# Block 2's mixing products as three fp32r products of split weights and inputs

## The reference, cut to what matters

```python
h = modulate(rmsnorm_2(x, norm1_g[l]), sh1, sc1)
a, naq, nak, nav, gq, gk, gv, gates = split_in(h @ w_in[l])
br_a = conv_branch(a, ...)                 # glu, 31-tap depthwise conv, layer norm, silu, @ w_conv_out
br_b = na_latent(naq, nak, nav, ...) @ w_na_out[l]      # windowed attention, 8 heads
br_c = gqa_latent(q, k, gv, ...) @ w_gqa_out[l]         # grouped attention, 8 heads
x = x + g1 * merge(br_a, br_b, br_c, gates, w_out[l])   # sum of sigmoid(gate) * branch, @ w_out
x = x + g2 * swiglu(modulate(rmsnorm_2(x, norm2_g[l]), sh2, sc2), w_ffn_in[l], w_ffn_out[l])
```

## Time and profile before

| | us |
|---|---|
| runs (3) | median 3305.6, 3302.19 to 3306.99 |
| the profiled execution | 3307.56 |
| its span, first to last instruction | 3305.8 |
| mean granted TensorE clock | 0.962 |

### The profile page before, as it was taken

How to read it: one execution, slowest core, us unless ns; L and a number is a source line. 1 busy time by engine, 2 the same in 40 slices (tenths; PEclk the granted TensorE clock), 3 DMA queues, 4 the chain that set the end, 5 groups by cost and what they waited for, 6 DMA issues and landing times.

```text
span 3305.8 us, 36114 instructions
## 1 busy us (share of the span) xinstructions
PE 3086.5 (93%) x15078; PEld 2396.2 (72%) x15078; DVE 1602.2 (48%) x2403; ACT 1034.4 (31%) x1473; POOL 360.8 (11%) x331
## 2 busy tenths in 40 slices
PE   6999888999999988999799899999999989899998
PEld 5888667888888766788565355545888867767787
DVE  6832223585863132387354244314757626253474
ACT  4422113344431211354200234312434420253342
POOL 2300010131310000032000230010000000230000
PEclk9999889999999888999899999999999999999999
DMA  6545553455554555356222120113554533322453
GB/s 197 185 148 156 191 166 128 141 187 181 180 191 121 177 167 165 102 179 203 77 90 77 55 71 28 51 51 102 183 186 158 184 106 115 107 71 89 140 179 103
DMA packets 433640, 444.98 MB, mean 135 GB/s; under 512 B 13487, under 2 KB 425256, under 8 KB 433478
## 3 DMA queue, kind: packets, MB, share of 16 engines
q1 hardware_dynamic: 427936, 434.86, 41.1%
q0 software_dynamic: 2400, 5.40, 0.7%
q10 hardware_dynamic: 3142, 2.41, 0.2%
HBM read 441.46 MB, written 1.17 MB: 134 GB/s over the span
## 4 chain that ended last, share of the span: by engine, by line
PE 83%; issue 7%; DVE 5%; ACT 4%; POOL 1%; ACTq 0%; DMA 0%; POOLq 0%; DVEq 0%
PE bank L1325 26%; PE bank L1374 20%; PE bank L1326 13%; PE bank L1384 11%; PE bank L1317 3%; PE bank L1468 1%; PE bank L1669 1%; PE bank L1475 1%; PE bank L1679 1%; PE bank L1545 1%; PE bank L1407 1%; DVE lower L1792 1%; PE bank L1305 1%; PE bank L1534 1%; POOL R L867 1%
## 5 line engine op out<-in xcount | busy, mean ns | idle before, releaser
L1325 PE MATMUL bank<-h_pair,upper 128*128 128x512 f32 x2464 | 876.8, 401 | 37.0 <-DVE h_pair L1823 18.7
L1792 DVE TENSOR_TENSOR lower<-ring,upper 128x2048 fp32r<-128x2048 f32 (+1 forms) x238 | 570.8, 2401 | 290.2 <-ACT upper L922 290.2
L1326 PE MATMUL bank<-h_pair,lower 128*128 128x256 f32 x2464 | 693.5, 281 | 0.0
L1374 PE MATMUL bank<-hT,ring 128*128 128x256 f32 (+1 forms) x2176 | 614.6, 441 | 12.4 <-DVE hT L1782 11.4
L922 ACT ACTIVATE upper<-ring 128x2048 fp32r<-128x2048 f32 (+1 forms) x238 | 441.7, 1863 | 502.8 <-PE bank L1326 502.8
L1325 PEld LDWEIGHTS bank<-h_pair,upper 128*128 128x128 f32 x2464 | 467.5, 190 | 152.6 <-issue 34.1
L1374 PEld LDWEIGHTS bank<-hT,ring 128*128 128x128 f32 x2176 | 413.8, 192 | 207.8 <-issue 151.4
L1326 PEld LDWEIGHTS bank<-h_pair,lower 128*128 128x128 f32 x2464 | 469.9, 191 | 0.2
L1325 PE MATMUL bank<-hid_pair,upper 128*128 128x512 f32 x1232 | 432.1, 396 | 0.0
L1384 PE MATMUL bank<-ring,hT 128*128 128x256 f32 (+2 forms) x1600 | 369.0, 395 | 30.2 <-ACT Q L994 19.7
L1384 PEld LDWEIGHTS bank<-ring,hT 128*128 128x128 f32 x1600 | 314.6, 205 | 80.4 <-issue 35.7
(11 more groups left out here) (256 smaller groups left out, 2722.8 us busy)
## 6 DMA issues: line engine op xcount, KB each, us to landing
ring<-in_w_ffn_in SPq DMA_DIRECT2D x154, 1024.0 KB, 5.1
ring<-in_w_ffn_out SPq DMA_DIRECT2D x56, 1024.0 KB, 5.2
ring<-in_w_in SPq DMA_DIRECT2D x50, 1024.0 KB, 5.3
ring<-in_w_mix_in SPq DMA_DIRECT2D x48, 1024.0 KB, 5.4
ring<-in_w_mod SPq DMA_DIRECT2D x48, 1024.0 KB, 5.4
ring<-in_w_ffn_out SPq DMA_DIRECT2D x28, 768.0 KB, 4.5
ring<-in_w_mix_out SPq DMA_DIRECT2D x16, 1024.0 KB, 5.3
ring<-in_w_out SPq DMA_DIRECT2D x8, 1024.0 KB, 5.3
```

Of the source, the lines that this page charges most:

```text
L1325: pe.matmul(bank[:, 0:2 * T], up[:, cols], x_pair.rearrange("p e t -> p (e t)"), start=first, stop=False)
L1326: return pe.matmul(bank[:, 0:T], low[:, cols], x_pair[:, 0, :], start=False, stop=last)
L1374: mm = pe.matmul(bank[b][:, 0:nT], w[:, c:c + 128], rhs(k), start=k == 0, stop=k == n_k - 1)
L1792: dve.tensor_tensor(f.lower(p)[:, 0:n], slot[:, 0:n], f.upper(p)[:, 0:n].bitcast(F32), ALU.subtract)\
```

## The change

Every product of block 2's mixing with a weight (projections, gates, branches, `w_out`) becomes three fp32r products: upper weight x upper input, upper x lower, lower x upper. Norm sums, scores, PV and the turnings stay as they are.

- **Weights.** The 35 mixing pieces of a layer use raw slots 0 to 2 (piece n in slot n % 3); slots 3 to 5 hold the upper parts of the same three. Piece n is loaded when piece n-3 has been used. ScalarE rounds a piece into its upper slot (`split2_up`), then the lower part is left in the raw slot by VectorE, or, for pieces 7 to 16, by GpSimd (`split2_low`, `LOW_ON_POOL`). On ScalarE and VectorE the split of piece n+3 stands behind their work on the item that piece n fills (`piece_done`); the first three are split before the norm's root.
- **Inputs.** The normed input h is scaled (VectorE), shifted and rounded (ScalarE) and its lower part left by VectorE, chunk by chunk; item 0 takes the chunks in order, for both banks. The convolution branch's silu is computed twice, rounded and whole, and subtracted. Attention's results are evicted rounded by ScalarE (`o_up_ready`), and VectorE subtracts them from the PSUM bank (`out_low`, for unit i-4 after the mask of unit i), which now gives `o_ready`. `y2` is rounded by ScalarE and subtracted by VectorE, chunk by chunk, before `w_out`.
- **Loads.** SyncE's order is now one list, `PIECES`, for the whole kernel; outside the mixing the slots go round six as before. The third probability buffer moves from `sq` to `caus`.

The core of the diff:

```diff
+MIX2_SLOTS = 3
+MIX2_PIECES = sum(n for _, n in PROJ2) + 6 * len(BRANCH2) + 4
+LOW_ON_POOL = range(7, 17)
...
+        for n, (name, i, end) in enumerate(pieces):
+            if n >= MIX2_PIECES:
+                add(name, i, layer, end, len(out) % NW)
+                continue
+            add(name, i, layer, end, n % MIX2_SLOTS)
+            up = MIX2_SLOTS + n % MIX2_SLOTS
+            out[-1].n, out[-1].up, out[-1].up_before = mixed, n % MIX2_SLOTS, held.get(up)
+            held[up] = end
+            mixed += 1
...
+            for piece in PIECES:
+                src, k, cols = source(piece.name, piece.i, piece.layer)
+                if piece.before is not None:
+                    ended(sp, piece.before)
+                sp.dma_start(slots[piece.slot][:, 0:k * cols].rearrange("p (k n) -> p k n", k=k), src)\
+                  .then_inc(landed[piece.slot], 16)
...
+        def low2_of(pos):
+
+            n = PIECES[pos].n
+            on_pool = n % MIX2_PIECES in LOW_ON_POOL
+            count = sum((m % MIX2_PIECES in LOW_ON_POOL) == on_pool for m in range(n + 1))
+            return (low2_on_pool if on_pool else low2_on_dve), count
+
+        def split2_low(eng, pos):
+
+            piece = PIECES[pos]
+            eng.wait_ge(up2_ready, piece.n + 1)
+            eng.tensor_tensor(lowers[piece.slot], slots[piece.slot], uppers2[piece.up].bitcast(F32), ALU.subtract)\
+               .then_inc(low2_of(pos)[0], 1)
...
+                for n in LOW_ON_POOL:
+                    split2_low(pool, pos + n)
...
+            def split2_up(pos):
+
+                piece = PIECES[pos]
+                has_landed(act, pos)
+                if piece.up_before is not None:
+                    ended(act, piece.up_before)
+                act.activation(uppers2[piece.up], slots[piece.slot], ACT.Copy).then_inc(up2_ready, 1)
...
-            def glu_gates(item, nT, n_items):
+            def glu_gates(item, nT, n_items, pos):
 
                 for n in range(n_items):
                     it = item + n
                     filled(act, it)
                     act.activation(glu[it % 2][:, 0:nT], pair[it % 2][0][:, 0:nT], ACT.Sigmoid)\
                        .then_inc(glu_ready, 1)
+                    if n % 2:
+                        split2_up(pos + n - 1 + MIX2_SLOTS)
+                        split2_up(pos + n + MIX2_SLOTS)
...
+                def piece_done(n, pos=pos):
+
+                    if n + MIX2_SLOTS < MIX2_PIECES:
+                        split2_up(pos + n + MIX2_SLOTS)
...
+                    piece_done(13 + 6 * b + i)
...
-                    act.activation(cout[:, c, 0:nT], cout[:, c, 0:nT], ACT.Silu,
-                                   bias=pcol("conv_ln_b_2", KC2 * layer + c),
-                                   scale=pcol("conv_ln_g_2", KC2 * layer + c)).then_inc(ln_ready, 1)
+                    for dst in (cout_up, cout):
+                        ins = act.activation(dst[:, c, 0:nT], cout[:, c, 0:nT], ACT.Silu,
+                                             bias=pcol("conv_ln_b_2", KC2 * layer + c),
+                                             scale=pcol("conv_ln_g_2", KC2 * layer + c))
+                    ins.then_inc(ln_ready, 1)
+                piece_done(17)
+                piece_done(18)
...
-                        dst = naoT if kind.startswith("na") else goT
+                        dst = nao_up if kind.startswith("na") else go_up
                         r = slice(HD * (h % 2), HD * (h % 2) + HD)
                         q0, n = (T, T) if kind.endswith("c") else (P * qt, P)
-                        out_unit((unit), i - 3, dst[r, h // 2, q0:q0 + n], r, n)
+                        out_unit((unit), i - 3, dst[r, h // 2, q0:q0 + n], r, n, o_up_ready)
                     done = woven_before(layer, i, "gate")
                     if done:
                         sigmoid_gates(*done)
+                    done = woven_before(layer, i, "branch")
+                    if done and done[1] % 2:
+                        piece_done(17 + 6 * done[0] + done[1] // 2)
                 unit += len(units)
+                piece_done(29)
+                piece_done(30)
+                for m in range(KD):
+                    act.wait_ge(y2_ready, 16 * layer + 8 + m + 1)
+                    act.activation(y2_up[:, m, 0:nT], y2[:, m, 0:nT], ACT.Copy).then_inc(y2_up_ready, 1)
+                piece_done(31)
...
+            def products3(out, w, w_cols, x, first, last):
+
+                (up, low), (x_up, x_low) = w, x
+                for n, (w_, x_) in enumerate(((up, x_up), (up, x_low), (low, x_up))):
+                    mm = pe.matmul(out, w_[:, w_cols], x_, start=first and n == 0, stop=last and n == 2)
+                return mm
...
+            def glu_pieces(item, pos, nh, n_pairs, h_before):
+
+                for n in range(n_pairs):
+                    w = [split2(pos + 2 * n), split2(pos + 2 * n + 1)]
                     for j in range(2):
-                        bank = start_item(it + j)
-                        for e in range(2):
-                            for k in range(KD):
-                                mm = pe.matmul(bank[e][:, 0:nh * T], w[e][:, k * PC + 128 * j:k * PC + 128 * (j + 1)],
-                                               hT[:, 0:nh, k, :], start=k == 0, stop=k == KD - 1)
+                        bank = start_item(item + 2 * n + j)
+                        first = n == 0 and j == 0
+                        order = [(e, k) for k in range(KD) for e in range(2)] if first else \
+                                [(e, k) for e in range(2) for k in range(KD)]
+                        for e, k in order:
+                            if first and e == 0:
+                                pe.wait_ge(h_ready, h_before + k + 1)
+                            c = k * PC + 128 * j
+                            mm = products3(bank[e][:, 0:nh * T], w[e], slice(c, c + 128), h2(nh)(k), k == 0,
+                                           k == KD - 1)
...
+                def h2_low_part(c):
+
+                    dve.wait_ge(h2_up_ready, layer * KD + c + 1)
+                    for hf in range(2):
+                        ins = dve.scalar_tensor_tensor(out=h2_low(c, hf, 1).rearrange("p a t -> p (a t)"),
+                                                       in0=h2_whole[hf][:, c, :], scalar=mod[:, layer, c, hf:hf + 1],
+                                                       in1=h2_up[:, hf, c, :].bitcast(F32), op0=ALU.add,
+                                                       op1=ALU.subtract)
+                    ins.then_inc(h_ready, 1)
+
+                for c in range(KD):
+                    for hf in range(2):
+                        ins = dve.scalar_tensor_tensor(out=h2_whole[hf][:, c, :], in0=xT[:, hf, c, :],
+                                                       scalar=mod[:, layer, 8 + c, hf:hf + 1],
+                                                       in1=root[:, hf * T:(hf + 1) * T], op0=ALU.mult, op1=ALU.mult)
+                    ins.then_inc(h_scaled, 1)
+                    if c:
+                        h2_low_part(c - 1)
+                h2_low_part(KD - 1)
...
+                def out_low(j, unit=unit, units=units):
+
+                    kind, h, qt = units[j]
+                    up, low = (nao_up, nao_low) if kind.startswith("na") else (go_up, go_low)
+                    r = slice(HD * (h % 2), HD * (h % 2) + HD)
+                    q0, n = (T, T) if kind.endswith("c") else (P * qt, P)
+                    dve.wait_ge(o_up_ready, unit - UNITS1 + j + 1)
+                    dve.tensor_tensor(low[r, h // 2, q0:q0 + n], M[3][r, 0:n], up[r, h // 2, q0:q0 + n].bitcast(F32),
+                                      ALU.subtract).then_inc(o_ready, 1)
+
+                for i in range(len(units) + 4):
                     if i < len(units):
                         na = units[i][0] == "na"
                         mask_unit((unit), i, units[i][0], chain, bias_n if na else None)
                         bias_n += na
-                    if i >= 1:
+                    if i >= 4:
+                        out_low(i - 4)
+                    if 1 <= i < len(units) + 1:
                         scale_unit((unit), i - 1, units[i - 1][0], chain)
+                    done = woven_before(layer, i, "gate")
+                    if done:
+                        piece_done(13 + 6 * done[0] + done[1])
                     done = woven_before(layer, i, "branch")
                     if done:
                         gated_branch(*done)
+                        if done[1] % 2:
+                            piece_done(17 + 6 * done[0] + done[1] // 2)
...
+                for m in range(KD):
+                    dve.wait_ge(y2_up_ready, KD * layer + m + 1)
+                    dve.tensor_tensor(y2_low[:, m, 0:nT], y2[:, m, 0:nT], y2_up[:, m, 0:nT].bitcast(F32),
+                                      ALU.subtract).then_inc(y2_split, 1)
+                for n in range(4):
```

(3 more changed lines are left out.)

302 lines of the change are left out of this document (168 added, 134 removed).

## The result

| | before | after |
|---|---|---|
| median of 4 runs, us | 3303.89 (3298.53 to 3306.99) | 3460.16 (3459.18 to 3464.08) |
| ratio, 95% interval | | 1.0477 [1.0459, 1.0495] |
| the profiled execution, us | 3307.56 | 3460.09 |
| its span, us | 3305.8 | 3458.3 |
| mean granted TensorE clock | 0.962 | 0.908 |

The account below looks back on a forecast made before the run. TensorE, busy 93% of the span, was taken as the limit. Stage terms of +34 us in layer 0 and +75 in layer 1 made +109 on 3307.6, so 3417, or 3415 as a median; range 3335 to 3460.

Parts of the forecast that it names:

- the twelve terms: Six stages of each layer's mixing, glu to output: +34 us in layer 0, +75 in layer 1.
- the price of the products: Mixing's weight products on TensorE: 0.23 us per 512-column fp32r product, 0.12 per 256-column one, 139 us off TensorE.
- the bounds of 0.215 and of 0.19 a weight load: Product price limits: 0.215 adds 23 us of gain; 0.19 takes 155 us away (rival at 3520, chance 0.05).
- the lock between GpSimd and VectorE: Beside the convolution, GpSimd's subtractions cost VectorE 4.3 us a piece, 43 us for ten.
- T + 142 and T + 111: Convolution's end in layers 0 and 1, counted from item 3's end T; stage changes of -9 and 0 us.
- the rival of 3495: GpSimd gets no turn during the convolution, so pieces from 7 on come after it: +51 and +29 us, chance 0.07.
- `out_low` behind the mask behind the subtraction: Attention, when a gate piece ends: PV waits for VectorE's `out_low`, 14.4 against 9.7 on the step's clock, 4.7 us lost.
- The rival in which `out_low` is in time: Attention: `o_ready` comes before TensorE finishes its step's work; 121 us less than forecast, 3294, chance 0.08.
- the slow-clock term: Attention: one 3.3 us stretch at half clock after each stall, 1.7 us lost, +14 us a layer.
- its 4.15: Attention steps with nothing woven in: score, mask, `out_low`, PV in line take 4.15 us instead of 3.04.
- the range's upper end: Whole kernel: the stated range, 3335 to 3460, ended at 3460 and left 0.20 out.
- the forecast's own band: Whole kernel: 3360 to 3465, from 1.06 to 5.0 us of lock per piece, none to two slow stretches per stall; chance 0.66.

Follow-up runs that it names:

- e7: e3 with all GpSimd subtractions moved to VectorE between convolution taps, and seven pieces' copies and subtractions moved behind steps that others wait for: 3217.13 us, ratio 0.9747.
- e4: The changed kernel with GpSimd writing zeros into the lower parts of pieces 7 to 16 instead of subtracting: 3440.36 us.
- e1: The changed kernel with VectorE taking `out_low` of unit i-4 ahead of the mask of unit i instead of behind it: 3363.93 us.
- e2: The changed kernel with VectorE's subtraction of a gate or branch piece in attention one step later, `out_low` still behind the mask: 3340.64 us.
- e3: The changed kernel with both attention reorderings, `out_low` ahead of the mask and the piece's subtraction one step later: 3313.63 us.
- e5: The changed kernel with unused products added on TensorE, two in each plain attention step and four in each step with a gate's stall: 3408.81 us.
- e8b: e7 with one unused product more in each plain attention step: 3214.06 us, ratio 0.9742 to before.

## Why the prediction was right or wrong

**Right: what bounds each stage, and the side.** Slower had 0.92. Ten of the twelve terms are within 4.2 us of what was measured; the two others are the attention of the two layers.

**Right: the price of the products.** 0.230 us for 512 columns in the chain of after, 0.120 for 256 in that of e7; the bounds of 0.215 and of 0.19 a weight load are both out. The Trainium skill (TensorE: Matmul & The Clock Gate, Back-to-back issue gap) has, for the gap of an isolated product, N/2.4 + 2.5 ns, 0.216 and 0.109 us; by the rows it is 6 and 10% dearer here.

**Right: the lock between GpSimd and VectorE.** 4.3 us a piece taken, 4.3 measured (0.89 of 4.85 us, where 0.84 of 5.0 had been taken); projections of T + 142 and T + 111 worked out, 142.2 and 109.3 found. e4 takes the lock away and the time with it. GpSimd got its turns, so the rival of 3495 was wrong.

**Right: `out_low` behind the mask behind the subtraction.** 4.7 us of idle time worked out, 4.3 to 4.6 measured in layer 0 and 3.8 to 4.0 in most of layer 1; e1 takes the mask out of it and the stall is shorter by the mask, e2 takes the subtraction out and it is gone. The rival in which `out_low` is in time did not occur in after, but e2 with e1 is that case: e3 has 3313.6. The rival's own 3294 was 20 too good, for the reason given under e3: the plain steps wait for more than `out_low`.

**Wrong: the size of the slow-clock term.** The step that failed is "Per stall one stretch at half clock follows ... 1.7 us lost: +14 a layer", and, next to it, that the plain steps have none. It was sized from a window of 3.3 us at 0.50 after one isolated wait. After a stall of 4.5 us in layer 0's attention the clock stays at 0.50 for 10 us (7 to 10 us in layer 1): the stalled step itself is 1.0 us longer and the one behind it 3.2 to 3.4, together 4.2 to 4.4 where 1.7 was taken. And in the plain steps, which idle 0.9 to 1.2 us each, it stays at 0.50 for 65 us (layer 0) and 72 us (layer 1) on end, and each pays 2.1 us on top of its 4.15. Why a wait of 4.5 us has 10 us at 0.50 behind it here, and one of 5.4 us only 3.3 in the earlier trace rows, no run shows. Where the 66 us are by which the attention exceeded the forecast, from the steps of before and after:

| us over the forecast | layer 0 | layer 1 |
|---|---|---|
| plain steps | 14 | 20 |
| steps with woven products, stalled or behind a stall, and the tail | 8 | 11 |
| the step between plain and woven | 5 | 4 |
| the first two steps | 2 | 1 |

The second row is small for its mechanism since the number of stalls was off as well: I counted eight gate stalls a layer, and between first and last score there are six in layer 0 and seven in layer 1, while the pieces of the branches, counted at 0 and 2 us, cost about 9 and 6. e5 gives back 52 of the 66 us by added work alone. The other 14 us I have not taken apart; the branch pieces, whose steps take 7.4 to 8.5 us in e5 too, are a part of them.

The bound was wrong for the same reason as the value: the range's upper end took two such stretches for each stall, and none for the plain steps. It ended at 3460, and the result is 3460.16. That the forecast's own band went on to 3465 and so holds the result is luck: it has room for dearer locks, which did not come, and none for the plain steps' slow clock, which did.

**Elsewhere** the small errors were mostly on the dear side: layer 1's glu by 4 us, norm and the way to the first score by 5 in both layers together, the projections by 1. Three sums of the prediction are off without moving the forecast much: the gain on TensorE splits into 93 and 46 us, not 89 and 50; by the rule of the Trainium skill named there it would be 185, not 183; and in layer 1 two steps of 5.45 us (6.03 less 8 products' 0.07) and a stall of 4.7 are 15.6 us, not 15.1, which adds 4 us over eight pieces, though the stalls there were then 0.8 us shorter than taken. The 12 us by which block 1 was shorter in the profile of after hid a part of the attention's miss: with block 1 as in before, the miss of the whole would have been 57 us instead of 45.

## What to carry to other kernels

Where an engine gives a buffer back that the busiest engine waits for, look at what is queued ahead of that instruction, and let no wait for a DMA or for another engine's large copy stand there: two such orders (e3) cost 155 us here, and a few more (e7) 70, while the products they served had become 139 us cheaper. Idle time on TensorE is to be priced with the clock that follows it, and once per step if it recurs in each step: take the price from rows with recurring waits, or bound it by doubling all TensorE work of the stretch. Idle time that recurs does not always bring the slow clock: in before's plain steps, with 1.0 us in every second one, it was 0.95. If a change meant to save TensorE time leaves its busy time nearly unchanged while the mean granted clock falls, that is the sign; a run with added products in the idle time tells the clock from the wait.

## What the runs showed of the hardware

- In before, after an isolated wait of 5.4 us, the granted clock was 0.50 (the 1.2 GHz level) over the 3.3 us of the earlier trace rows; in after, behind stalls of 4.5 us that came every four steps in layer 0, over 10 us each time; in steps with 0.9 to 1.2 us idle of 6.2, over 65 and 72 us without a break, and in e2, with no stall ahead of them, over 61 us. With 1.8 us of added products in each such step TensorE's rows are those of the full 2.4 GHz, and the step fell from 6.2 to 4.3 us (e5). In e8b, where the clock was at 0.50 for only 10 and 7 us of such steps, added products changed neither that nor the time. The Trainium skill (TensorE: Matmul & The Clock Gate, A second HAM failure mode: psum-queue depth-cycling) tells of short idle times between groups of products that make the clock change between its levels again and again. In the plain steps here it does not change but stays at the lower one.
- A GpSimd subtraction of 2048 elements (4.85 us) beside the convolution's multiply-adds takes 4.3 us from VectorE. A GpSimd memset of the same tile (1.81 us) takes nothing that shows.
- The end of block 1, whose instructions are the same in all kernels here, differs by up to 14 us between the profiles of ten kernels (1584.0 to 1598.1), more than the whole spread of the runs of after (3459.18 to 3464.08). With one profile of each, no run shows whether it goes with the kernel or with the execution.
